# The low-rank attention core and the choice of keys inside the gates' product, the sparse core beside a branch product

## The reference, cut to what matters

```python
z = rmsnorm(x, attn_norm_g) @ w_in           # 1024 -> 3492 columns
a_q, a_k, a_v, i_q, i_k, i_w, c_q, c_kv, k_r, g = split_cols(z, IN_SIZES)
# branch a, sparse: 8 heads of 64, one shared key and value head
score = sum_h iw_h * relu(iq_h @ ik.T / 8)   # 4 index heads, causal
_, sel = lax.top_k(score, 128)               # 128 keys of each query
y_a = softmax(a_q @ a_k[sel].T / 8 + rel_bias) @ a_v[sel]
# branch b, low-rank: 8 heads of 64 + 32 rotated columns
q = rmsnorm(c_q) @ w_uq; k, v = split(rmsnorm(c_kv) @ w_ukv)
y_b = softmax(rope(q) @ rope(k).T / sqrt(96)) @ v
merged = sigmoid(g0 + b0) * (y_a @ w_branch_a) + sigmoid(g1 + b1) * (y_b @ w_branch_b)
x = x + merged @ w_out
```

## Time and profile before

| what | value |
|---|---|
| median of 3 runs | 2323.83 us (2320.15 to 2326.82) |
| the profiled execution's own time | 2321.61 us |
| span of the profile | 2319.8 us |
| mean granted clock of PE | 0.94 of full |
| PE busy | 2108.7 us (91%) |
| DVE busy | 1421.7 us (61%) |
| ACT busy | 848.2 us (37%) |
| POOL busy | 119.1 us (5%) |

### The profile page before, as it was taken

The page is one execution under the profiler, slowest core; times in us unless marked ns, Lnnn a source line. Parts: engine busy times, 40 slices in busy tenths (PEclk is TensorE's granted clock), DMA queues, the critical chain, the costliest instruction groups (busy, mean ns, idle before and its releaser), DMA issues.

```text
span 2319.8 us, 25409 instructions
## 1 busy us (share of the span) xinstructions
PE 2108.7 (91%) x10180; PEld 1633.5 (70%) x10182; DVE 1421.7 (61%) x2430; ACT 848.2 (37%) x1397; POOL 119.1 (5%) x97
## 2 busy tenths in 40 slices
PE   3999769999998988886999999899889999999998
PEld 2655558888886875565888887677655588888886
DVE  6799768856845446646762563667767664633632
ACT  2333434433433245533442442423363433422331
POOL 1000120000011000011000001100000001000000
PEclk9999779999998999997999999899895899999999
DMA  7321235565531221011323222222110022332321
GB/s 281 112 73 37 101 108 192 196 201 173 196 103 55 72 65 37 28 47 32 108 92 103 96 87 95 70 82 69 32 37 2 1 83 90 100 93 90 105 94 64
DMA packets 61749, 214.74 MB, mean 93 GB/s; under 512 B 6848, under 2 KB 7744, under 8 KB 61632
## 3 DMA queue, kind: packets, MB, share of 16 engines
q1 hardware_dynamic: 61632, 213.12, 28.2%
HBM read 211.00 MB, written 2.10 MB: 92 GB/s over the span
## 4 chain that ended last, share of the span: by engine, by line
PE 78%; DVE 14%; ACT 3%; issue 2%; POOL 2%; DMA 1%; POOLq 0%; DVEq 0%; SPq 0%; ACTq 0%
PE bank L281 22%; PE bank L283 22%; PE bank L282 22%; PE bank L286 10%; DVE C L938 4%; PE bank L680 2%; DVE wlo L313 1%; POOL part L415 1%; DMA raw<-in_mod_w 1%; DVE raw L541 1%; DVE steps L733 1%; DVE tmp L499 1%; DVE Hl L491 1%; POOL small L447 1%; DVE tmp L462 1%
## 5 line engine op out<-in xcount | busy, mean ns | idle before, releaser
L281 PE MATMUL bank<-Hh,whi 128*128 128x512 f32 x1632 | 662.2, 406 | 72.4 <-DVE wlo L313 16.7
L282 PE MATMUL bank<-Hl,whi 128*128 128x512 f32 x1632 | 647.4, 397 | 0.0
L283 PE MATMUL bank<-Hh,wlo 128*128 128x512 f32 x1632 | 646.6, 396 | 0.0
L313 DVE TENSOR_TENSOR wlo<-stg,whi 128x1024 fp32r<-128x1024 f32 (+1 forms) x309 | 372.1, 1209 | 410.1 <-ACT whi L308 409.2
L308 ACT ACTIVATE whi<-stg 128x1024 fp32r<-128x1024 f32 (+1 forms) x309 | 314.0, 1026 | 448.6 <-PE bank L283 442.1
L281 PEld LDWEIGHTS bank<-Hh,whi 128*128 128x128 f32 x1632 | 313.7, 192 | 164.6 <-issue 37.5
L283 PEld LDWEIGHTS bank<-Hh,wlo 128*128 128x128 f32 x1632 | 313.7, 192 | 67.8
L282 PEld LDWEIGHTS bank<-Hl,whi 128*128 128x128 f32 x1632 | 314.5, 193 | 66.6 <-issue 3.4
L283 PE MATMUL bank<-HIDh,wlo 128*128 128x512 f32 x352 | 140.4, 399 | 0.0
L282 PE MATMUL bank<-HIDl,whi 128*128 128x512 f32 x352 | 138.7, 394 | 0.0
L281 PE MATMUL bank<-HIDh,whi 128*128 128x512 f32 x352 | 138.0, 392 | 0.0
(11 more groups left out here) (284 smaller groups left out, 2625.6 us busy)
## 6 DMA issues: line engine op xcount, KB each, us to landing
raw<-in_mod_w SPq DMA_DIRECT2D x96, 512.0 KB, 4.6
stg<-in_ffn_in SPq DMA_DIRECT2D x88, 512.0 KB, 4.1
stg<-in_ff SPq DMA_DIRECT2D x64, 512.0 KB, 3.5
stg<-in_ffn_out SPq DMA_DIRECT2D x40, 512.0 KB, 3.6
stg<-in_cm_w SPq DMA_DIRECT2D x24, 512.0 KB, 4.4
stg<-in_gates SPq DMA_DIRECT2D x16, 512.0 KB, 3.5
stg<-in_z_ch SPq DMA_DIRECT2D x12, 512.0 KB, 3.5
stg<-in_w_k SPq DMA_DIRECT2D x8, 512.0 KB, 3.5
```

The source lines that it names most:

```text
L281: pe.e.matmul(out_, l[0], r[0], start=start, stop=False, skip_group_check=True)
L282: pe.e.matmul(out_, l[0], r[1], start=False, stop=False, skip_group_check=True)
L283: return pe.e.matmul(out_, l[1], r[0], start=False, stop=stop, skip_group_check=True)
L313: dve.e.tensor_tensor(wlo[j % NW][:, 0:n * c], stg[j % NSTG][:, 0:n * c], whi[j % NW][:, 0:n * c].bitcast(F32), ALU.subtract).then_inc(*w_ ...
```

## The change

- The weight blocks of the low-rank heads come between those of the gates; the order of products on PE becomes: four `z_ch` groups, eight `gates` groups, the last two `z_ch` groups (`AQ`), `br_b`, `br_a`, `w_out`.
- All index products and weighted sums (`scores_*`) run within gates group 0, two at a time in two banks; the 48 rounds of the choice (`best_dve`) run on DVE within groups 1 to 7, one for each advance.
- `mla` runs within groups 1 on, one item for each advance (8 a group, 37 steps). It has two score banks and one output bank. `w_uv` and `heads(0)` come at the end of group 0, `heads(1)` to `heads(3)` in the middle of groups 1 to 3.
- The rotation of a head is one DVE product, one ACT copy and two POOL operations. DVE's product of a head waits until POOL has finished the head before, since they share one tile.
- The output of `mla` goes to `YB` and is split into halves after the `AQ` groups.
- `dsa` runs within the four `br_b` groups: 4 advances a group, 16 of its 37 steps; the rest follows alone. It has two score banks and one bias bank. `br_a` and the merge come last.

```diff
     gemm("z_ch", 0, DT, [0, 256, 512, 768])
+    for g in range(8):
+        heads = [("w_uq", 0, 2, 256 * g, 256), ("w_uk", 0, 1, 128 * g, 128)] if g < 4 else []
+        halves = [("gates", k, 4, 256 * g, 256) for k in (0, 4)]
+        plan += [*halves, ("w_uv", 0, 1, 0, 512), *heads] if g == 0 else [halves[0], *heads, halves[1]]
     gemm("z_ch", 0, DT, [1024, 1280])
...
+    gemm("br_b", 0, 4, range(0, D, 256))
+    gemm("br_a", 0, 4, range(0, D, 256))
...
-            GEN, OB = [4, 7], {"mla": [5, 6], "dsa": [6, 7]}
+            OB = {"mla": [5], "dsa": [6, 7]}
+            HEAD_BANKS = [(0, 1, 0), (0, 1, 0), (2, 6, 2), (0, 1, 0)]
...
+                for n in range(12):
+                    qb, h, N = n // 4 + 1, n % 4, P * (n // 4 + 2)
+                    rows, b = slice(64 * (h % 2), 64 * (h % 2) + 64), (3, 7)[n % 2]
+                    open_bank(b, [(act_done, ("relu", n))])
...
+            def heads_beside(work, g):
+                if g == 0:
                     yield
+                work(g)
+                yield
...
+            mla = Core("mla", [mla_item(2 * j + n // 4, n % 4) for j in range(4) for n in range(8)], [3, 7], [4], sq[0:3],
+                       tmp[0:3], stat_b, 1)
+            dsa = Core("dsa", [dsa_item(h, qb) for qb in range(4) for h in range(H)], [2, 3], [4], sq, tmp[0:3], stat_a, 1)
...
             def heads_dve(j):
+                if j == 0:
+                    next_block(dve, "w_uv", 0)
                 next_block(dve, "w_uq", 0)
                 for x in range(2):
                     dve.wait_ge(*gemm_done["mq", j, x])
+                    if 2 * j + x:
+                        dve.wait_ge(*pool_done["mrot", j - 1 + x, 1 - x])
+                    dve.e.tensor_tensor(sq[3][64:96, :], banks[HEAD_BANKS[j][x]][96:P, :], ROT[96:P, :], ALU.mult).then_inc(
+                        *dve_done.up(("mturn", j, x)))
+                next_block(dve, "w_uk", 0)
+
+            def heads_pool(j):
+                for x in range(2):
+                    pool.wait_ge(*act_done["mqr", j, x])
+                    pool.wait_ge(*act_done["rot"])
+                    pool.e.tensor_tensor(pair_buf[x][64:96, :], pair_buf[x][64:96, :], ROT[64:96, :], ALU.mult).then_inc(*pool_done.up())
+                    pool.wait_ge(*dve_done["mturn", j, x])
+                    pool.wait_ge(*pool_done.now)
...
+                    pool.e.tensor_tensor(QM[64:96, 2 * (j % 2) + x, :], pair_buf[x][64:96, :], sq[3][64:96, :], ALU.add).then_inc(
+                        *pool_done.up(("mrot", j, x)))
...
+                lat = latents_pe()
+                pe.within[:] = [lat]
                 gemm("z", "z_ch", HX("z"), 0, DT, 2, z_by, 4)
+                rotate_banks([0, 1, 2, 6])
+                steps = mla.tensor()
+                for g in range(8):
+                    pe.within[:] = [lat, scores_pe()] if g == 0 else [steps]
+                    pe.beside[:] = [heads_beside(heads_pe, g)] if g < 4 else []
+                    gemm("gt", "gates", HX("z"), 0, DT, 1, lambda m: [(dve_done, ("gt", m))], 2 * g)
+                pe.within[:] = []
+                all_of(steps)
                 gemm("aq", "z_ch", HX("z"), 0, DT, 2, lambda m: [(dve_done, ("aq", m))])
+                rotate_banks([0, 1])
+                steps = dsa.tensor(None, lead_dsa(lambda qb: steps_pe("ds", 4 * FIRST[qb], 4 * (FIRST[qb + 1] - FIRST[qb]), Tb, [5])))
+                pe.within[:] = [steps]
+                gemm("bb", "br_b", lambda q: (YBh[:, q, :], YBl[:, q, :], dve_done["yb", q]), 0, 4, 4, lambda m: [(dve_done, ("mb", m))])
                 pe.within[:] = []
+                all_of(steps)
+                rotate_banks([0, 1, 2, 3, 4])
+                gemm("ba", "br_a", lambda q: (YAh[:, q, :], YAl[:, q, :], dve_done["ya", 6 + q // 2]), 0, 4, 4,
+                     lambda m: [(dve_done, ("ma", m))])
...
+                steps, top = mla.vector(nothing_to_close), best_dve()
+                for g in range(8):
+                    dve.within[:] = [lat, scores_dve()] if g == 0 else [steps, top]
+                    dve.beside[:] = [heads_beside(heads_dve, g)] if g < 4 else []
+                    if g == 1:
+                        dve.wait_ge(*dve_done["score", 11])
+                    beside_gemm(dve, "gates", 0, DT, 1, gt_evac, 2 * g)
```

More of the change, by code:

```diff
@@ L1615, in branch_stage @@
             pa = ExitStack()
[L1616 to L1617 removed]
+            B2 = [sb("B2a", [P, H, 3 * P], F32, pa), sb("B2b", [P, H, S], F32, pa)]
+            AQ = sb("AQ", [P, 4, S], F32, pa)
             pa.close()
@@ L1705, in best_act @@
                 yield
+                for n in range(12):
+                    N = P * (n // 4 + 2)
+                    act.wait_ge(*core_done["dots", n])
+                    if n > 2:
+                        act.wait_ge(*dve_done["score", n - 3])
+                    act.e.activation(tmp[n % 3][:, 0:N], banks[(3, 7)[n % 2]][:, 0:N], ACT.Relu, scale=0.125).then_inc(
+                        *act_done.up(("relu", n)))
+                    if n % 2:
+                        yield
                 act.wait_ge(*pool_done["causal"])
@@ L1708, in best_act, with best_dve @@
+            def best_dve():
                 for qb in range(1, 4):
                     N = P * (qb + 1)
-                    for h in range(4):
-                        act.wait_ge(*core_done["dots", qb, h])
-                        if qb > 1:
-                            act.wait_ge(*dve_done["score", qb - 1, h])
-                        act.e.activation(tmp[h][:, 0:N], banks[5][:, 0:N], ACT.Relu, scale=0.125).then_inc(*act_done.up(("relu", qb, h)))
-                        yield
-                    for _ in range(17):
-                        yield
@@ L1812, in heads_pe @@
             def heads_pe(j):
+                if j == 0:
+                    jb = next_block(pe, "w_uv", 0)
+                    hi, lo = block_parts(jb)
+                    for tb in range(4):
+                        b, c = (0, 1)[tb % 2], slice(tb * P, (tb + 1) * P)
+                        open_bank(b, [(act_done, ("vb", tb))])
+                        pe.wait_ge(*w_lo[jb])
+                        pe.wait_ge(*dve_done["cql", 2])
+                        mm3(banks[b][:, :], (CQh[:, 2, c], CQl[:, 2, c]), (hi[:, 0, :], lo[:, 0, :]), True, True).then_inc(
+                            *gemm_done.up(("uv", tb), *([("block", jb)] if tb == 3 else [])))
                 jb = next_block(pe, "w_uq", 0)
@@ L1833, in heads_act @@
             def heads_act(j):
+                if j == 0:
+                    next_block(act, "w_uv", 0)
+                    for tb in range(4):
+                        act.wait_ge(*gemm_done["uv", tb])
+                        act.wait_ge(*dve_done["cql", 2])
+                        act.e.activation(VB[:, tb, :], banks[(0, 1)[tb % 2]][:, :], ACT.Copy).then_inc(*act_done.up(("vb", tb)))
                 next_block(act, "w_uq", 0)
@@ L2038, in b_evac @@
                         *dve_done.up(("mg", t)))
-                for j in range(4):
-                    beside_gemm(dve, "br_a", 0, 4, 1, a_evac, 2 * j)
-                    beside_gemm(dve, "br_b", 0, 4, 1, b_evac, 2 * j)
+                beside_gemm(dve, "br_a", 0, 4, 4, a_evac)
                 def x_evac(m):
@@ L2118, in gpsimd @@
                 pool.wait_ge(*norm_done["sum", "ckv"])
+                for j in range(4):
+                    heads_pool(j)
                 pool.wait_ge(*dve_done["ya", 7])
```

312 lines of the change are left out of this document (127 added, 185 removed).

## The result

The changed kernel takes 2335.27 us (median; 2327.77 to 2342.23, 16 runs) against 2323.68 (2316.85 to 2329.48, 16 runs) beside it: ratio 1.0049, interval 1.0036 to 1.0061. It is slower by 0.5%, where I had forecast 2304 and a range up to 2328. The profiled execution has a span of 2334.1, so its trace may be read for the median.

What follows compares the result with a forecast made beforehand. The prediction took PE, and places where PE waits for DVE, to bound the kernel. From 2321.6 us it subtracted 9 (gates, low-rank core, `AQ`) and 10.5 (sparse core): 2302.1, forecast 2304 by the median's level; range 2284 to 2328.

Steps and rivals of the forecast that it cites:

- step 1: Gates group 0 with the index products: 20.9 us, of which index products 10; with `w_uv` and `heads(0)`, ending at 1549.0.
- Step 2: Gates groups 1 to 4 beside the low-rank core: sum 115.5 us, ending at 1665.5.
- 0.72+1.05+0.1 = 1.9: End of a gates group: next block's low half waits 1.9 us for a high half behind a sigmoid in ACT's list.
- The last rival: POOL and DVE take turns: 16 POOL operations of 1.39 us, 22.2, 4 already counted; 2322, no change; chance 0.07.
- Step 3: Gates groups 5 to 7 and `AQ`: DVE bounds; end at 1729 against 1738 before, a gain of 9 us.
- Step 4: Sparse core beside `br_b`: 68.5 us to step 16, sum 135, a gain of 10.5; with no loss 126, gain 19.5.
- two nearly equal engines in turn lose some and the clock starts low: Sparse core's first 16 steps beside `br_b`: 7 us added to 51 for PE and DVE alternating and a low starting clock.
- Step 5: `br_a` takes 21.8 us on PE as before; DVE's merge falls some 6 us behind, hidden by the first `w_out` blocks.
- Slower, by the handing over: The 32 items in groups 1 to 4: late handovers between engines cost 1.0 us a step, giving 2336; chance 0.12.
- Slower, by the clock: Sparse core's 16 steps beside `br_b` stay at 1.2 GHz, adding 33 to 36 us, giving 2338; chance 0.12.
- what would show it: Trace signs: gates groups 1 to 3 at 28 to 32 us, DVE over 85% busy, first 16 sparse steps under 70 us.
- PE bounds everywhere: Both gains, in the gates with low-rank core and the sparse core, come in full, 22 + 19.5: 2282; chance 0.17.

Runs made afterwards that it cites:

- e8: Changed kernel with only DVE's low half moved to mid-block, behind the third step, in gates groups 1 to 7 and `br_b`; ACT's high half unmoved: 2298.6 us.
- e3: Changed kernel with the weight split moved mid-block (ACT's high half behind the first step, DVE's low behind the third), gates groups 1 to 7 and `br_b`: 2297.3 us.
- e6: Changed kernel with the weight split moved to mid-block on ACT and DVE in `br_b` only; the gates' groups keep the old order: 2322.7 us.
- e4: Changed kernel with both the mid-block weight split (gates groups 1 to 7, `br_b`) and the 16 sigmoids moved beside the `AQ` groups: 2298.3 us.
- e1: Changed kernel with the sparse part undone: the sparse core runs alone, then `br_b` alone: 2336.8 us.
- e7: Changed kernel with the mid-block weight split in gates groups 1 to 7, and the sparse core run alone before `br_b`: 2317.0 us.
- e2: Changed kernel with the gates' 16 sigmoids moved behind the low-rank core, beside the `AQ` groups: 2315.0 us.
- e5: Changed kernel with the weight split moved to mid-block on ACT and DVE in gates groups 1 to 7 only; `br_b` keeps the old order: 2312.2 us.
- e9: Changed kernel with the 16 gates computed by Exp in place of Sigmoid, in the same places, so gate values differ: 2321.4 us.
- e10: Kernel before the change, with the weight split moved to mid-block in all eight groups of its gates' product: 2324.4 us.
- e11: Changed kernel with the mid-block weight split (gates groups 1 to 7, `br_b`) and two alternating rotation buffers, so DVE needn't wait for POOL: 2292.1 us.

## Why the prediction was wrong

From the forecast of 2304 to 2335.3 are 31.3 us. In order:

| part | forecast | measured | difference |
|---|---|---|---|
| step 1: to the end of group 0 | 1541.4 | 1535.2 | -6.2 |
| `w_uv`, `heads(0)`, groups 1 to 4 | 124.1 | 133.3 | +9.2 |
| groups 5 to 7 | 46.3 | 52.8 | +6.5 |
| `AQ` | 17.2 | 17.4 | +0.2 |
| sparse core to step 16 | 68.5 | 88.5 | +20.0 |
| its rest | 66.6 | 64.1 | -2.5 |
| `br_a` | 21.8 | 22.4 | +0.6 |
| behind it | | | +3.6 |

**Step 1 was mis-sized, to the good side, by an error of reading.** I put ten groups in the 121.7 us of the earlier trace rows. But group 0 of after shows where a group begins (its first and last product matmul, and the first of `w_uv`):

```profile
1514.99 0.79 PE L279 MATMUL bank<-Hh,whi 128*128 128x512 f32 x1
...
1532.94 0.40 PE L281 MATMUL bank<-Hh,wlo 128*128 128x512 f32 x1
1534.68 0.51 PE L279 MATMUL bank<-whi,CQh 128*128 128x512 f32 x1 [1.34 <-DVE GT L1981]
```

These are 48 product matmuls with the index products between them, and they begin 5.8 us ahead of my cut; in before, too, 24 of the ten groups' 480 matmuls lie ahead of 1520.5. The index products with their waits so cost 18.3 before (121.7 - 456 x 0.227), not 12.9, and 18.1 - 10.9 = 7.2 after, not 10.

**Step 2 failed in the term "0.72+1.05+0.1 = 1.9"**, the wait at a group's end, and in the sentence "ACT has under 19 us in such a group and is covered". Three things were missing. The wait comes at each block's boundary, twice a group, not once: eight times in groups 2 to 5, 32.5 us. It is longer: 4.61 in the example, with both sigmoids, a table load of 1.28 and an output copy of 0.59 ahead of the high half. And it isn't a matter of DVE's sum: without the waits I had summed 23.1 and 25.2 us of DVE in groups 2 and 3, and it was busy 21.2 and 23.7, but PE idles behind the soft step that is queued behind the low half. I had named what is queued behind the wait for POOL and not what is queued behind this one. e8 shows that this is the fault, e3 what it costs with the clock: with the split moved, groups 1 to 4 take 33.7, 30.0, 31.6 and 23.4. An engine that is busy 57 to 60% of a group, as ACT is (19.3 to 21.2 us), is not "covered" if what it makes is needed at one moment.

Right in kind in this step: the wait for POOL, priced at 3.3, took 8.3 in 4, 2.1 each; and the second of the two rotation operations on POOL takes longer beside a DVE low half, and the low half as well:

```profile
1622.85 1.29 POOL L1895 TENSOR_TENSOR QM<-diag,sq 32x512 f32<-32x512 f32 x1
1624.11 1.28 POOL L1890 TENSOR_TENSOR part<-part,ROT 32x512 f32<-32x512 f32 x1
1624.97 1.50 DVE L311 TENSOR_TENSOR wlo<-stg,whi 128x1024 fp32r<-128x1024 f32 x1
1625.53 2.07 POOL L1895 TENSOR_TENSOR QM<-part,sq 32x512 f32<-32x512 f32 x1
1626.39 2.30 DVE L311 TENSOR_TENSOR wlo<-stg,whi 128x1024 fp32r<-128x1024 f32 x1
```

2.07 in place of 1.29 on POOL, and 3.71 for two low halves of which a pair without POOL beside it takes 2.36: 1.35 us of DVE in this group, near the 1.0 that I took from the earlier trace rows. Each of the three ends as if it had begun to run when the other engine's instruction ended: the first low half 1.08 us after POOL's 1625.39, the POOL operation 1.13 after the low half's 1626.47, the second low half 1.09 after POOL's 1627.60. So the trace agrees with the Trainium skill, "SBUF — State Buffer", section "Who interferes with whom", that the two exclude each other for whole instructions. An operation that begins late in the other's is lengthened by the rest of it only., too, is no evidence against it: of that POOL operation 1.22 us were left when the DVE one began, which took 1.02 longer. The last rival failed in another term: it took all 16 POOL operations to collide. Only DVE's low halves, with both inputs in SBUF (the on-chip memory that is not a bank), were lengthened, and all 16 POOL operations together took 22.95 us, about 2.5 over 16 of 1.28.

**Step 3 failed for group 5** (26.2 for 18.1), where the core's last items meet two such boundaries, with waits of 4.4 and 5.3 us; "1.0 for the core's tail" was a guess, and in e3 the group takes 20.1. After's 26.2 holds 2.7 of clock as well (e6 has 23.5 with the same order). Groups 6 and 7, without a core, were right: 17.2 and 9.4 for 17.9 and 10.3.

**Step 4 failed in its 7 us for "two nearly equal engines in turn lose some and the clock starts low".** 88.5 for 68.5. DVE isn't full (55.9 of 88.5). In e3 the same work takes 71.2: the 17.3 between are 7.1 idle and 10.2 clock, and what e3 lacks are the pauses at the boundaries of `br_b`'s blocks. A second term was mis-sized: in these 71.2 PE is busy 64.3 at a clock of 0.98, where I had summed some 54.5 (4.5 at the start and 50). The 7 us that I added for other reasons covered most of that, by luck. The third and fourth query blocks were right. In e3 the whole of the step takes 134.4 (71.2, 32.7 and 30.5) against 145.6 before, a gain of 11.2 where I had 10.5; without loss my own terms (10.5, 50 and 66.6) give 127.1 and a gain of 18.5, not 126 and 19.5.

**Step 5** held: `br_a` 22.4, and the merge is not seen. The 3.6 behind it are a stretch in which PE had no pause and yet a clock of 0.66. It begins within 24 matmuls of one column each (rows of the timeline, then the stretch):

```profile
1969.33 0.95 PE L284 MATMUL bank<-ones,part 128*128 128x1 f32 x8
1970.14 2.33 PE L284 MATMUL bank<-ones,sq 128*128 128x1 f32 x16
```

```profile
1970.00:1980.00 10.00, 10.00 (x40) 8.23 (x39) 2.17 (x6) 0.65 (x1) 1.02 (x1) 0.66 0.17 54
```

No step of the change works there. At the same place of the program, 56.2 us after the first matmul of `w_out`, e4 and e8 have 0.66 too (1934.0 to 1944.0 and 1935.5 to 1945.5), e1 and e7 0.83, and before, e2, e3, e5, e6, e9, e10 and e11 1.00. From the first matmul of `w_out` to the end of the span it is 420.3 or 420.4 us with 0.66, 418.8 with 0.83 and 417.1 or 417.2 in the changed kernels with 1.00. So it belongs to no edit, and what decides whether it comes is open.

**The rivals.** "Slower, by the handing over" gave 2336 with a chance of 0.12, and 2336 is nearly what came, but its place was wrong: not 1 us in each of 32 steps but some 2 to 3 us of idle PE and about as much of clock at each boundary, and more of it in the sparse core than in groups 1 to 4. "Slower, by the clock" was wrong as put: beside `br_b` the clock was 0.83, not 0.5. Of "what would show it", DVE busy over 85% and the 70 us for the first 16 steps failed, and so named the two steps that fell; groups 2 and 3 took over 33 us, my own sign of being wrong; group 5 was not near 18, and `AQ` ended 218.3 us after 1520.5, not 205 to 210. "PE bounds everywhere" (2282) is 10 us from e11.

That e3 lies near 2304 is not the forecast come true: it has other waits than I had reckoned with, and several errors in it cancel (step 1 put too high, PE's work beside `br_b` too low).

## What to carry to other kernels

When work that hands over between three engines is laid within a product, look for what else stands in the same lists at the same places: the product's own upkeep (here the split of the next weight block) becomes a link in the chain if it waits for another engine. Make such upkeep in the middle of a block, where its input has long been ready and the work queued behind it is not yet due. For each added wait, price what is queued behind it and the slow clock after it, not only the wait; and sum by engine only after asking at which moment each result is needed.

## What the runs showed of the hardware

- A change of activation function between sigmoid and exp costs ACT 1.283 us each way, visible as an instruction of its own, with 0.02 us to its neighbours on either side (the timeline above).
- After a pause of PE of 1.8 to 3.0 us the product's matmuls mostly take 0.63 in place of 0.39 for about 3 us (from 1647.9 in the timeline above): in after behind eight of the nine such pauses that a product's matmuls follow closely, but not behind the one of 1.86 at 1560.7. In the changed kernel the clock took about as much as the pauses themselves (from after to e3: 19.6 us by clock, 19.4 idle).
- A stretch without any pause may also be granted 0.66 (1970 to 1980 above). In five of the eleven traces of changed kernels, after's among them, a low stretch stands at that place, behind 24 matmuls of one column, and in six it doesn't.
- In three cases a DVE operation with both inputs in SBUF and a POOL one took turns: in the rows of 1624 to 1629 above each ends 1.08 to 1.13 us after the other's end, though it had begun 0.42, 0.94 and 1.21 us before it.
